# The first two modulation vectors by 512 columns in turn, six tiles multiplied between their pieces, and the rest of the opening in periods of four ring places

## The reference, cut to what matters

```
mod = silu(c) @ w_ada + b_ada              # c: [1, 2048], w_ada: [2048, 6 * 2048]
sh1, sc1, gt1, sh2, sc2, gt2 = split(mod, 6)
h = rmsnorm(x, norm1_g) * (1.0 + sc1) + sh1
p = h @ w_in                               # lora columns, then k, r, v (3 * 1024), then pool
p = p + mu * (shift_by_one_token(p) - p)   # for the lora, k, r, v columns
...                                        # decay, gates, key norm, then the wkv recurrence over 16 heads
```

## Time and profile before

| what | value |
|---|---|
| median of 3 runs | 2819.8 us (2817.44 to 2823.07) |
| the profiled execution's own time | 2819.87 us |
| its span, first to last instruction | 2818.1 us |
| PE busy | 2697.9 us, 96% |
| DVE, ACT, POOL busy | 1825.9, 1260.3, 143.7 us |
| granted TensorE clock, mean | 0.979 of full |
| HBM read | 551.29 MB, 196 GB/s over the span |

### The profile page before, as it was taken

The page is one execution under the profiler, slowest core; times in us unless marked ns, Lnnn a source line. Parts: engine busy times, 40 slices in busy tenths (PEclk is TensorE's granted clock), DMA queues, the critical chain, the costliest instruction groups (busy, mean ns, idle before and its releaser), DMA issues.

```text
span 2818.1 us, 47810 instructions
## 1 busy us (share of the span) xinstructions
PE 2697.9 (96%) x17516; PEld 2224.6 (79%) x17516; DVE 1825.9 (65%) x2529; ACT 1260.3 (45%) x1712; POOL 143.7 (5%) x149
## 2 busy tenths in 40 slices
PE   5799999989999999999999999999999999999998
PEld 0357667777888888888888888887878888888887
DVE  0455565666877777755576676678577777776554
ACT  1432222244555555544443355643455555554443
POOL 1001100321000000010100000000100000000000
PEclk7799999999999999999999999999999999999999
DMA  9776655434555555555555544444545555555553
GB/s 401 286 293 252 236 229 227 173 115 162 187 193 188 184 193 192 185 205 208 196 185 180 192 163 153 162 164 166 192 161 182 189 183 187 185 183 205 206 197 134
DMA packets 82701, 554.73 MB, mean 197 GB/s; under 512 B 8496, under 2 KB 8624, under 8 KB 17840
## 3 DMA queue, kind: packets, MB, share of 16 engines
q1 hardware_dynamic: 81888, 550.21, 53.1%
q10 hardware_dynamic: 720, 3.21, 0.3%
HBM read 551.29 MB, written 2.10 MB: 196 GB/s over the span
## 4 chain that ended last, share of the span: by engine, by line
PE 86%; DVE 6%; DMA 3%; ACT 2%; issue 2%; DVEq 0%; SPq 0%; ACTq 0%
PE bank L516 52%; PE bank L517 26%; DMA raw<-in_stream_dram 3%; PE bank L559 2%; DVE wlo L1460 1%; PE bank L683 1%; DVE yb L1476 1%; PE bank L697 1%; PE bank L693 1%; DVE zmat L1695 0%; DVE t L1583 0%; DVE yb L2065 0%; PE bank L775 0%; PE bank L781 0%; PE bank L768 0%
## 5 line engine op out<-in xcount | busy, mean ns | idle before, releaser
L516 PE MATMUL bank<-act,whi 128*128 128x512 f32 x4976 | 1785.2, 403 | 24.4 <-DVE act L1497 20.9
L517 PE MATMUL bank<-act,wlo 128*128 128x256 f32 x4976 | 1396.5, 281 | 0.0
L516 PEld LDWEIGHTS bank<-act,whi 128*128 128x128 f32 x4976 | 940.7, 189 | 279.3 <-issue 38.6
L1460 DVE TENSOR_TENSOR wlo<-raw,whi 128x1024 fp32r<-128x1024 f32 x846 | 1035.2, 1232 | 177.8 <-ACT whi L1034 171.5
L1034 ACT ACTIVATE whi<-raw 128x1024 fp32r<-128x1024 f32 x846 | 883.5, 1052 | 438.4 <-PE bank L517 409.0
L517 PEld LDWEIGHTS bank<-act,wlo 128*128 128x128 f32 x4976 | 944.8, 190 | 3.6 <-issue 3.4
L516 PE MATMUL bank<-ff,whi 128*128 128x512 f32 x1408 | 493.2, 393 | 1.0 <-DVE wlo L1460 1.0
L517 PE MATMUL bank<-ff,wlo 128*128 128x256 f32 x1408 | 392.8, 279 | 0.0
L516 PEld LDWEIGHTS bank<-ff,whi 128*128 128x128 f32 x1408 | 263.8, 187 | 64.6 <-DVE wlo L1460 1.6
L517 PEld LDWEIGHTS bank<-ff,wlo 128*128 128x128 f32 x1408 | 263.8, 187 | 0.0
L1476 DVE TENSOR_REDUCE joined<-bank 128x256 f32<-128x512 f32 x179 | 123.4, 691 | 212.2 <-PE bank L517 212.0
(11 more groups left out here) (236 smaller groups left out, 1518.4 us busy)
## 6 DMA issues: line engine op xcount, KB each, us to landing
raw<-in_stream_dram SPq DMA_DIRECT2D x519, 1024.0 KB, 4.8
x<-in_x_dram SPq DMA_DIRECT2D x1, 2048.0 KB, 14.4
lora_w<-in_lora_dram SPq DMA_DIRECT2D x1, 1536.0 KB, 11.6
pool_w<-in_pool_w_dram ACTq DMA_DIRECT2D x1, 1024.0 KB, 8.8
out_dram<-x SPq DMA_DIRECT2D x2, 512.0 KB, 2.8
out_dram<-x ACTq DMA_DIRECT2D x2, 512.0 KB, 3.0
catt<-in_att_dram ACTq DMA_DIRECT2D x1, 576.0 KB, 3.4
par<-in_params_dram SPq DMA_DIRECT2D x1, 541.5 KB, 3.3
```

What stands on the lines that cost most here:

```text
L516: nc.tensor.matmul(tile_bank(t), wh, flat(pair[:, kt]), start=starts and n == 0, stop=False)
L517: mm = nc.tensor.matmul(small_half(t), wl, pair[:, kt, 0], start=False, stop=stops and last)
L1460: nc.vector.tensor_tensor(wlo[:, k % RING], raw[:, r % RING, 8 * (k % 2):8 * (k % 2) + 8], whi[:, k % RING].bitcast(F32), ALU.subtract).th ...
```

## The change

**Units.** The two vectors sh1 and sc1 are no longer made one after the other. They are made in four units u of 512 columns each. A unit has eight pieces of 1 MB: parts 0 to 3 for sh1, 4 to 7 for sc1, each with 4 x 128 rows of w_ada and 512 columns, so rows of 2 KB. After part 3 and part 7 ACT copies the sum, PE multiplies it with `pick` into four columns (`unit_columns`), DVE adds the bias, and after sc1 the fill of the unit's four rows follows. x is loaded ahead of all pieces.

**Six tiles.** The three lora tiles and the first three tiles of the opening are accumulated in six banks at once, row by row (`six_rows`): 4 rows x 6 tiles = 24 products for each unit. Their six weight pieces come in the order of loads between a unit's parts 5 and 6 (two, one, two and one). The products of unit u - 1 stand in unit u behind part 2 (12) and behind part 4 (12); those of the last unit stand behind it.

**Rest of the opening.** Ten halves (10 steps m), with one or two ada pieces after each: 16 as before. Where the order before had one weight piece in three loads, it now has one in four. The joins of the six tiles, their corrections and their activations stand at the head of the opening on DVE and ACT. `preparation` is spread over the steps by OPEN_PREPARATION. Segment 0 leaves the function `segment`, and on DVE the cut of half 24 is moved from segment 1 ahead of `preparation(14)`.

```diff
...
+UNITS, FIRST_SIX = KT // 4, 6
...
+def open_chunks(m):
+    return 2 if m % 2 or m == OPEN_STEPS - 2 else 1
 def raw_order():
-    w = FIRST_CHUNK["wkv"]
-    order = [("w", c) for c in range(w + 2)]
-    c, a = w + 2, 0
-    for s in range(NGROUP):
+    order = []
+    for u in range(UNITS):
+        order += [("first", 8 * u + q) for q in range(6)]
+        order += [("w", c) for c in ((0, 1), (2,), (3, 4), (5,))[u]]
+        order += [("first", 8 * u + q) for q in (6, 7)]
+    order += [("w", FIRST_SIX), ("w", FIRST_SIX + 1)]
+    c, a = FIRST_SIX + 2, 0
+    for m in range(OPEN_STEPS):
+        if m in (0, 2, 4, 6):
+            order.append(("w", c))
+            c += 1
+        for _ in range(open_chunks(m)):
+            order.append(("ada", a))
+            a += 1
...
+LORA_AT = {1: (0, 1), 2: (2,), 3: (3,)}
+OPEN_PREPARATION = {3: (1, 4), 6: (7,), 7: (8,), 8: (9, 10), 9: (14,)}
...
+            def load_unit(r):
+                u, part = divmod(ORDER[r][1], 8)
+                first = KT * (part // 4) + 4 * (part % 4)
+                src = stream[first:first + 4, :, 4 * P * u:4 * P * u + 4 * P].rearrange("k p n -> p k n")
+                dst = raw[:, r % RING].rearrange("p (k four) n -> p k (four n)", four=4)
+                sp.dma_start(dst, src).then_inc(raw_full[r % RING], 16)
...
+            for r in range(FIRST_LOADS):
+                if r >= RING:
+                    freed(r - RING)
+                if ORDER[r][0] == "first":
+                    load_unit(r)
+                else:
+                    load_first(r)
...
-                if r == ADA0 + RING - 1:
+                if r == FIRST_LOADS + 1:
                     sp.dma_start(lora_w[:], lora_in).then_inc(lora_loaded, 16)
...
-            for v in range(2):
-                for kt in range(KT):
-                    ada_chunk(KT * v + kt, KT * v + kt)
-                if v == 0:
-                    ada_turn(0)
...
+            def unit_part(u, part):
+                r = FIRST_PLACE[8 * u + part]
+                pe.wait_ge(raw_full[r % RING], 16 * (r // RING + 1))
+                h = part % 4
+                if h == 0 and u + part:
+                    pe.wait_ge(ada_copied, 2 * u + part // 4)
+                src = raw[:, r % RING].rearrange("p (k four) n -> p k (four n)", four=4)
+                for k in range(4):
+                    mm = nc.tensor.matmul(ada[32 * k:32 * k + 32, :], crep[:, 4 * h + k], src[:, k],
+                                          start=h == 0, stop=h == 3, tile_position=(0, 32 * k))
+                mm.then_inc(ada_used, 1)
+            def unit_columns(w):
+                pe.wait_ge(ada_copied, w + 1)
+                if w:
+                    pe.wait_ge(columns, w)
                 else:
-                    pe.wait_ge(mod_ready, 1)
-                    ada_turn(1)
-            pe.wait_ge(mod_ready, 2)
-            stat("x0")
-            for n in range(2 * LORA_CHUNKS):
-                full_half("lora", n, 0, 0, "h1")
+                    pe.wait_ge(picked, 1)
+                for b in range(4):
+                    mm = nc.tensor.matmul(aux[:, b:b + 1], ada_row[:, b * P:(b + 1) * P], pick[:], start=True, stop=True)
+                mm.then_inc(ada_turned, 1)
...
+            def six_rows(u, rows):
+                pe.wait_ge(lo_ready, 2 * max(FOUR_CHUNK[u], TWO_CHUNK[u]) + 2)
+                for kt in rows:
+                    pe.wait_ge(a_ready, kt + 1)
+                    for j in (4, 5, 0, 1, 2, 3):
+                        if j < 4:
+                            k, b = 2 * FOUR_CHUNK[u] + j // 2, 4 * (j % 2) + kt % 4
+                        else:
+                            k, b = 2 * TWO_CHUNK[u] + j - 4, kt % 8
+                        mm = blocks_product(k, ("lora", j), [(b, kt)], act2, kt == 0, kt == KT - 1)
+                        if kt % 4 == 3 and j in (1, 3) or kt % 8 == 7 and j >= 4:
+                            mm.then_inc(half_used, 1)
+            for u in range(UNITS):
+                for part in range(8):
+                    unit_part(u, part)
+                    if part == 2 and u:
+                        six_rows(u - 1, (4 * u - 4, 4 * u - 3))
+                    if part == 3:
+                        unit_columns(2 * u)
+                    if part == 4 and u:
+                        six_rows(u - 1, (4 * u - 2, 4 * u - 1))
+                    if part == 4 and u == 0:
+                        stat("x0")
+                unit_columns(2 * u + 1)
+            six_rows(UNITS - 1, range(KT - 4, KT))
...
             def opening():
-                for n in range(16):
-                    full_half("wkv", n, 0, 0)
-                    for j in LORA_AT.get(n, ()):
+                placed = 0
+                for m in range(OPEN_STEPS):
+                    if m == 0:
+                        pe.wait_ge(tile_sum, 1)
+                    full_half("wkv", OPEN_DONE + m, 0, 0, free=m == 0)
+                    for j in LORA_AT.get(m, ()):
                         if j == 0:
                             pe.wait_ge(lora_loaded, 16)
                             pe.wait_ge(lora_act, 3)
+                            pe.wait_ge(tile_sum, FIRST_SIX)
                         lora_decay(j)
-                    if 5 <= n <= 8:
-                        lora_gate(n - 5)
-                    ada_chunk(ADA_PLACE[n], ADA0 + n)
-                    if n == 6:
+                    if 4 <= m <= 7:
+                        lora_gate(m - 4)
+                    for _ in range(open_chunks(m)):
+                        ada_chunk(ADA_PLACE[placed], ADA0 + placed)
+                        placed += 1
+                    if m == 5:
                         kk_step(0)
-                    if n == 14:
+                    if m == 9:
                         bonus_step(0)
...
+            for u in range(UNITS):
+                copy_unit(2 * u)
+                if u == 0:
+                    std("x0")
+                for c in ((0, 1), (2,), (3, 4), (5,))[u]:
+                    cut_hi(2 * c)
+                    cut_hi(2 * c + 1)
+                copy_unit(2 * u + 1)
+                unit_high(u)
...
+            def opening():
+                first = 2 * FIRST_CHUNK["wkv"] + OPEN_DONE
+                cut_hi(first)
+                cut_hi(first + 1)
+                lora_scaled(0)
+                lora_scaled(1)
+                cut_hi(first + 2)
+                lora_scaled(2)
+                act.wait_ge(token_shifted, 1)
+                nc.scalar.activation(lora_x[0:LORA, 0], lora_x[0:LORA, 0], ACT.Tanh).then_inc(lora_act, 1)
+                shifted_tile(0, 0)
+                lora_sigmoid(1)
+                shifted_tile(0, 1)
+                lora_sigmoid(2)
+                shifted_tile(0, 2)
+                for m in range(OPEN_STEPS):
+                    cut_hi(first + m + 3)
+                    if m % 2 == 1:
+                        shifted_tile(0, tile_at(0, OPEN_DONE + m))
+                    for j in LORA_AT.get(m, ()):
+                        lora_decay(j)
+                    if m == 4:
+                        decay_out(0)
+                        square_keys(0)
+                    if m == 5:
+                        key_norm(0)
+                copy_ada(2)
...
+            for u in range(UNITS):
+                unit_columns(2 * u)
+                if u == 0:
+                    reciprocal_std("x0")
+                for c in ((0, 1), (2,), (3, 4), (5,))[u]:
+                    cut_lo(2 * c)
+                    cut_lo(2 * c + 1)
+                unit_columns(2 * u + 1)
+                unit_normed(4 * u)
+                unit_normed(4 * u + 1)
+                for kt in range(4 * u, 4 * u + 4):
+                    if kt % 4 < 2:
+                        unit_normed(kt + 2)
+                    unit_low(kt)
...
+            def join_six(j):
+                if j >= 2:
+                    dve.wait_ge(token_shifted, j - 1)
+                dve.wait_ge(half_used, 2 * FIRST_SIX - (1 if j < 2 else 0))
+                halves = tile_bank(("lora", j)).rearrange("p (h t) -> p t h", h=2)
+                nc.vector.tensor_reduce(joined[:, j % 2], halves, AX.X, ALU.add).then_inc(tile_sum, 1)
...
+            def opening():
+                first = 2 * FIRST_CHUNK["wkv"] + OPEN_DONE
+                cut_lo(first)
+                cut_lo(first + 1)
+                join_six(0)
+                join_six(1)
+                lora_shifted(0)
+                join_six(2)
+                lora_shifted(1)
+                join_six(3)
+                lora_shifted(2)
+                cut_lo(first + 2)
+                join_six(4)
+                shifted_tile(0, 0)
+                join_six(5)
+                shifted_tile(0, 1)
+                shifted_tile(0, 2)
+                for m in range(OPEN_STEPS):
+                    cut_lo(first + 3 + m)
+                    if 5 <= m <= 8:
+                        j = m - 5
+                        dve.wait_ge(lora_mm, 5 + j)
```

(9 more changed lines are left out.)

178 lines of the change are left out of this document (97 added, 81 removed).

## The result

| | before | after |
|---|---|---|
| median | 2823.5 us (6 runs) | 2849.8 us (6 runs, 2841.3 to 2852.4) |
| ratio, with its 95% interval | | 1.0105 [1.0079, 1.0131] |
| profiled execution, its span | 2819.9, 2818.1 us | 2851.1, 2849.3 us |
| first products start | 215.37 us | 233.91 us |
| from there to the second group's products | 93.35 us | 99.68 us |

What follows compares the result with a forecast made beforehand. PE was taken to bound the kernel after the first stretch, to about 215 us. Six tiles' end 127.9, opening 89.4 and clock loss 4.8 put first products at 222.1, 6.7 us later: 2826 us, range 2814 to 2838.

Steps and rivals of the forecast that it cites:

- the hold of the ring in the units: In the units, product blocks between reads keep ring places too long and the load queue runs empty, about 5.5 us.
- Where the delay falls: In the units, the hold counts in units 1 and 2; in unit 3 it hits a load behind the vectors' last.
- Short rows at nothing: In the unit loads, rows of 2 KB cost nothing; 0.3 us on each of 32 would have added 10.
- P: Start of the first products after the opening, forecast at 222.1 us instead of 215.4.
- The tail and the last 24 products: At the units' end, 5.1 us from the last piece to the first product, then 10.8 us for 24 products.
- T: End of the six tiles after the units, forecast at 127.9 us (121 to 139).
- The ring periods: In the opening, each weight load waits for the previous weight's cuts; 89.4 us from the six tiles' end, clock loss excluded.
- The clock behind the gaps: In the opening, three idle gaps lower PE's clock for work on the chain, 1.6 us each, 4.8 in all.
- A: Rival: clock high in the units and after the gaps, 2815 to 2819 us; chance 0.23, taken with D's near end.
- B: Rival: short ring waits, PE bounds the opening and the full gain shows, products 20 us earlier, 2800 us; chance 0.10.
- D: Rival: stalls in units and opening cancel the 17.8 us saved, 2814 to 2825 us; no separate chance given.
- C: Rival: both product blocks of a unit run at half clock, products at 245 us, time 2849 us; chance 0.12.

Runs made afterwards that it cites:

- e10: The long-row kernel e1 with the products of units 0 to 2 left out except those releasing whi; last unit piece read at 113.1 us, no time given.
- e14: Kernel e10 with the weight pieces moved behind the eight parts of a unit; last unit piece read at 110.3 us, no time given.
- e1: The changed kernel with its first 38 pieces stored contiguously, so loads read rows of 8 KB; ratio to before 1.0083.
- e2: The kernel before the change with its 32 first pieces loaded in rows of 2 KB, 1 MB apart; ratio to before 1.0029.
- e3: The changed kernel with the opening's four weight pieces ahead of ada pieces 2, 5, 9 and 12 instead of 0, 3, 6 and 9; ratio to before 1.0040.
- e13: The kernel before the change with 2 KB rows as in e2, but a piece's rows within one contiguous 1 MB; pieces every 2.76 us, no time given.

## Why the prediction was wrong

- **The step that failed: the hold of the ring in the units.** I had "about 5.5 in all" for the empty queue, so the last unit piece at 112. It was read at 124.1: 18 us behind a full queue. (By my own working it should have been 2 x 3.3 = 6.6; the 5.5 has no working of its own.) The size of a block was right (5.6 forecast; 4.4, 6.2 and 5.9 measured). What I left out was the weight piece behind the blocks, whose cut waits on the second block; and I counted a block's hold only beyond the slack of four places, where, as I now read it, the other holds had used that slack up. With long rows e10 puts the blocks at 9.5, e14 the weight pieces at 2.8 and the rest at 4.2.
- **Where the delay falls.** I had it in units 1 and 2 alone, and in unit 3 on a load behind the last of the vectors. The reads were 4.1 us late before the first block of all (3.0 in e1, with long rows), and in unit 3 another 2.1 came on top (15.6 to 17.7). There the last unit piece goes into the place of part 4, which PE reads only behind the first block, so it was issued at 117.9.
- **Short rows at nothing** was the second term that failed. I wrote that a full queue hides a landing time. e2 shows that a full queue is exactly where they cost (0.27 us a piece, 9.7 us at P, the very 10 that I had named and not taken). In after the queue is full only at first, and the holds cover a part of it: 1.5 to 4.1 us in the starts, 7.0 to 8.4 in the medians.
- **The tail and the last 24 products**: 124.1 to 129.13 is 5.0 (forecast 5.1); the products end 9.9 later (10.8). Right. T came out at 139.1 instead of 127.9, 11.2 late, at the upper bound I had given and not taken.
- **The ring periods** were right: weight 9, 10 and 11 issued at T + 20, 38 and 59 (forecast 19.6, 36.0, 57.0), PE idle 2.7, 3.3, 4.0 and 5.1 for raw (forecast 4 to 6), SP 79.5 us for cuts. P at T + 94.8 against 89.4 + 4.8 = 94.2. e3 shows that the order of the loads is worth 17 us of it.
- **The clock behind the gaps** agrees inside the opening (the eight passes behind the four gaps took 1.63 to 1.93 us instead of 1.06), though no run prices the 4.8 alone. It stopped one wait too early. PE waits 2.94 us for the last preparation, which this very chain makes late; the products behind it run at the low clock and the segment pays 6.3 us. I took the end to move with P. The Trainium skill, page "TensorE: Matmul & The Clock Gate", section "HAM oscillation — how this bites in real kernels", has bursts between DMA waits start cold each time. The 5.89 us of the products against 3.44 before agree, though this wait is for DVE; the products of e3, 3.41 us behind a wait of 1.30, do not. I had used the rule on three gaps of the opening and not on the wait at its end.
- **Sum**: 6.7 forecast, plus 11.2 (T), 0.6 (T to P) and 6.3 (segment 1) is 24.8.
- **Rivals**: A, B and D are out. C gave the right time, 2849, by luck: its blocks at half clock never happened (4.4 to 6.2, not 7.7), and its P was 245 where 233.9 was measured. The 6.3 us of segment 1, and a median of before 3.6 us above the run it counted from, made up most of the rest. I gave it 0.12 and cut the range below it.

## What to carry to other kernels

When work is put between reads of a small ring, add up all that keeps a place (the block, the copy, and each piece's own consumer with what that one waits for in a second ring), along the whole unit. As I read these runs, slack is spent once; no run shows that by itself. In an in-order ring look at where each slow piece stands: moving four weight pieces by two or three places in the list of loads was worth 17 us. And the idle of 2.9 us right ahead of a long dense stretch cost 6.3 us more behind it: fill such a wait, or end the chain that makes it.

## What the runs showed of the hardware

- Loads of 1 MB in rows of 2 KB ran at 389 GB/s, in rows of 8 KB at 421, both with a full DMA share; rows 1 MB apart and side by side were alike (e2, e13). The Trainium skill, page "DMA: Bandwidth & Descriptors", section "Specifications", gives 512 B as the least transfer for line rate. These runs show 8% less at 2 KB than at 8 KB, so here the measurement decides.
- After 2.94 us of idle time PE was busy throughout at a clock of 0.76 (235 to 255 us of after, above). After 1.30 us, in e3, the window of the same place reads:

```profile
219.00:239.00 20.00, 19.88 (x302) 15.32 (x303) 12.97 (x18) 5.49 (x9) 5.99 (x4) 1.00 0.56 210
```
